# A two-layer hybrid decoder trunk on eight cores: attention summed in PSUM, the mixer's second half as one pipeline by tile, and the dense layer in two halves

## What is computed

```python
for layer in range(2):
    mod = silu(c) @ w_mod[layer] + b_mod[layer]          # 1024 x 6144, f32
    shift_m, scale_m, gate_m, shift_f, scale_f, gate_f = split(mod, 6)
    h = rms_norm(x, norm_mix) * (1 + scale_m) + shift_m
    q, k, v, rq, rk, rv, rg = split(h @ w_in[layer])     # 512 512 512 256 256 512 512
    # A: 8 heads of 64, three branches (window, dilation) = (128,1) (512,4) (2048,16)
    #    branch: p = exp(q k^T / 8 + bias); o = p v / sum(p); merged by softmax of log sum(p)
    # B: 4 heads, chunkwise retention in chunks of 128: inner + cross, state * decay + k^T v,
    #    GroupNorm per head, times silu(rg)
    x = x + gate_m * (concat(attn, ret) @ w_out[layer])
    h = rms_norm(x, norm_ffn) * (1 + scale_f) + shift_f
    f = swiglu(h, 1024 -> 2816 -> 1024)                  # layer 0, dense
        or top-2-of-8 experts swiglu(h, 1024 -> 3584 -> 1024)   # layer 1
    x = x + gate_f * f
```

## Time and profile before

| what | value |
|---|---|
| times of three executions | 4713.21, 4617.8, 4628.58 us |
| median | 4628.58 us |
| the profiled execution's own time | 4578.78 us |
| its span on the slowest core (core 0) | 4577.1 us |
| spans of the eight cores | 4534.5 to 4577.1 us |
| busy share of that span | PE 70%, DVE 37%, ACT 25%, POOL 17% |

### The profile page before, as it was taken

One profiled execution on the slowest core, in us unless ns is written; L12 is line 12 of the kernel. 1 busy time (PEld: TensorE's weight loads), 2 busy tenths in 40 slices (PEclk: granted clock), 3 DMA queues, 4 the chain that ended last, 5 costly groups with the idle time before them and its releaser, 6 DMA issues.

```text
span 4577.1 us, 59941 instructions; the slowest of 8 cores (4534.5 to 4577.1 us)
## 1 busy us (share of the span) xinstructions
PE 3189.4 (70%) x20346; PEld 1754.7 (38%) x20355; DVE 1694.2 (37%) x2545; ACT 1146.6 (25%) x2003; POOL 760.9 (17%) x668
## 2 busy tenths in 40 slices
PE   3677654556899966677455552669976788889876
PEld 1233343423343422333334222325543545455543
DVE  0488854333133335888544325112111212121211
ACT  2244432313110112444233032111111213021211
POOL 0100011120035460000111300201121111111120
PEclk9676666767899987766666775779998999999998
DMA  5311010013411122100110150897787969595966
GB/s 171 82 14 12 4 17 8 8 19 115 74 28 28 24 72 60 14 9 5 17 13 3 20 205 24 139 148 123 115 140 111 158 90 163 95 161 89 150 97 98
DMA packets 278861, 334.36 MB, mean 73 GB/s; under 512 B 67823, under 2 KB 205167, under 8 KB 278480
## 3 DMA queue, kind: packets, MB, share of 16 engines
q0 software_dynamic: 243696, 254.15, 37.7%
q1 hardware_dynamic: 34788, 75.30, 4.8%
HBM read 505.93 MB, written 36.96 MB: 119 GB/s over the span
## 4 chain that ended last, share of the span: by engine, by line
PE 51%; DVE 14%; DMA 13%; issue 9%; ACT 8%; POOL 3%; another core or an unknown queue 1%; DVEq 1%; ACTq 0%; POOLq 0%; SPq 0%; PEldq 0%
PE ps L1245 12%; PE ps L1273 10%; PE ps L931 7%; DMA s_w2s<-moe_w 4%; PE ps L450 3%; DMA s_ring<-moe_w 3%; POOL s_x L500 3%; PE ps L535 3%; PE ps L585 2%; DVE s_acc L707 2%; PE ps L680 2%; PE ps L657 2%; DVE s_hbf L477 1%; DVE s_acc L691 1%; ACT s_sa L1248 1%
## 5 line engine op out<-in xcount | busy, mean ns | idle before, releaser
L1245 PE MATMUL ps<-s_hgT,s_ring 128*128 128x0 bf16 (+1 forms) x5824 | 849.5, 307 | 228.4 <-DVE s_gT L1249 100.6
L1245 PEld LDWEIGHTS ps<-s_hgT,s_ring 128*128 128x128 bf16 x5824 | 552.9, 101 | 526.1 <-issue 293.2
L1249 DVE TENSOR_TENSOR s_gT<-ps,s_sa 128x384 bf16<-128x384 f32 (+1 forms) x364 | 233.0, 640 | 846.0 <-ACT s_sa L1248 798.9
L1273 PE MATMUL ps<-s_w2s,s_gT 128*128 128x512 bf16 x2072 | 460.0, 386 | 69.3 <-DMA s_w2s<-moe_w 68.9
L1248 ACT ACTIVATE s_sa<-ps 128x384 bf16<-128x384 f32 (+1 forms) x364 | 199.3, 556 | 527.0 <-PE ps L1245 484.2
L1273 PEld LDWEIGHTS ps<-s_w2s,s_gT 128*128 128x128 bf16 x2072 | 204.8, 99 | 321.9 <-issue 86.0
L931 PE MATMUL ps<-s_hT,s_w 128*128 128x512 bf16 x1408 | 307.0, 381 | 21.2 <-DMA s_w<-ffn_w 21.2
L450 PE MATMUL ps<-s_wm,s_cact_rep 128*128 128x512 f32 x384 | 191.7, 657 | 129.8 <-DMA s_wm<-w_mod 128.8
L1248 ACT ACT_TABLE_LOAD x56 | 71.8, 1283 | 755.5 <-PE ps L1245 746.0
L500 POOL TENSOR_TENSOR s_x<-s_x,s_tmpf 128x1024 f32<-128x1024 f32 x96 | 221.8, 2342 | 189.0 <-DVE s_tmpf L495 189.0
L594 DVE RECIPROCAL s_rsb<-s_rsb 128x512 f32<-128x512 f32 x64 | 214.5, 3351 | 91.8 <-ACT s_rsb L592 91.8
(11 more groups left out here) (219 smaller groups left out, 4354.8 us busy)
## 6 DMA issues: line engine op xcount, KB each, us to landing
s_ring<-moe_w POOLq DMA_DIRECT2D x112, 1024.0 KB, 18.5
s_w2s<-moe_w POOLq DMA_DIRECT2D x56, 1024.0 KB, 26.9
s_wm<-w_mod SPq DMA_DIRECT2D x24, 2048.0 KB, 9.4
s_w<-ffn_w POOLq DMA_DIRECT2D x10, 1024.0 KB, 10.8
s_x<-x SPq DMA_DIRECT2D x4, 2048.0 KB, 9.1
out<-s_x SPq DMA_DIRECT2D x4, 2048.0 KB, 7.9
s_wqkv<-w_in POOLq DMA_DIRECT2D x24, 256.0 KB, 4.4
s_w2s<-ffn_w POOLq DMA_DIRECT2D x5, 1024.0 KB, 8.5
```

The source lines that it names most:

```text
L1245: ins = e.matmul(o, lhsT=ring[s_][:, kc, j * 128:(j + 1) * 128], rhs=r, start=(kc == 0), stop=(kc == 7))
L1249: k.op("dve", lambda e: e.tensor_tensor(out=gT[:, fc, c0:c0 + width], in0=ps[:, bb, 0:width], in1=sa[z][:, 0:width], op=ALU.mult), reads=[ ...
L1273: ins = e.matmul(ps[:, b0 + hf, :], lhsT=gT[:, fc, b * 128:(b + 1) * 128], rhs=w2s[:, fc, hf * 512:(hf + 1) * 512], start=(fc == 0), stop= ...
```

## The change

The program is written anew from the setup to the router; the MoE's loop over expert tiles stays. Memory is no longer handed out by scopes with barriers: `place` puts each buffer at a fixed offset, and the helper makes it wait for whatever shared its bytes, so the barriers between stages are gone. x is not kept in SBUF. It is read and written by tile through DRAM (`load_x`, `residual`).

- **Setup.** Only the shift and scale of the first norm are computed ahead (8 loads of 1 MB, 32 f32 matmuls of 32 columns each, at four column places, L441). All 20 other blocks of w_mod are worked off on DVE inside layer 0's attention, eight [128x512] instructions a block (`mod_half`), and go through DRAM (`modscr`). The norm is one pipeline of square sum, apply, transpose.
- **Attention.** v is projected once for all heads in natural layout, laid beside a block of 64 ones per pair of heads, and the dilated copies are fetched through DRAM (`vscr`). Per head 19 batches of up to 512 columns: `scores`, exp, product in place, and `pv`, one matmul that yields 64 rows of p v and 64 rows of sums and accumulates all three branches in PSUM banks 0 to 3. `finish` forms the reciprocal as exp(-ln) on ACT, two instructions a bank, and one product on DVE. The projections of the next pair of heads are put between the batches, with the root as exp(-ln/2).
- **Mixer's second half.** One loop over tiles does project, rotate, transpose, state, inner, outer, GroupNorm, gate, transpose, output projection, residual, norm and transpose, each some iterations behind the one before. The mean of GroupNorm is taken out of the weights ahead (`wst`). For layer 1 the router's logits are in the same loop.
- **Dense layer.** Two halves of 1024 tokens: `up` for all 22 blocks, then `down` over all 22 accumulated in PSUM, followed by residual and norm. w1 and w3 are loaded twice, w2 once.
- **MoE.** The first tile always belongs to expert 0; its six ring buffers and seven down buffers are issued before the router's sorting.

```diff
@@ attention @@
-                            k.op("dve", lambda e: e.reciprocal(out=rsb[:, z, :], in_=rsb[:, z, :]), reads=[Brs[z]], writes=[Brs[z]])
+                k.op("act", lambda e: e.activation(out=rsb[:, y, :], in_=ps[:, 7, :], func=AF.Ln, bias=float(64 * EPS)), reads=[PB[7]], writes=[Brsb[y]])
+                k.op("act", lambda e: e.activation(out=rsb[:, y, :], in_=rsb[:, y, :], func=AF.Exp, scale=-0.5), reads=[Brsb[y]], writes=[Brsb[y]])
...
-                        k.op("dve", lambda e: e.tensor_tensor(out=dst, in0=dst, in1=pov, op=ALU.add), reads=[PB[ob], Bacc], writes=[Bacc])
+                for q, (lhs, bank, c0, d, n, o_) in enumerate(work):
+                    last = i == nb_ - 1 and all(w_[1] != bank for w_ in work[q + 1:])
+                    ins = e.matmul(ps[:, bank, c0:c0 + (n - 1) * d + 1:d], lhsT=lhs, rhs=pr[:, y, o_:o_ + n], start=False, stop=last)
...
+        def finish(c, hh):
+            num = slice(64 * hh, 64 * hh + 64)
+            den = slice(64 - 64 * hh, 128 - 64 * hh)
+            for bank in range(4):
+                y = bank % 2
+                k.op("act", lambda e: e.activation(out=rec[num, y, :], in_=ps[den, bank, :], func=AF.Ln), reads=[PB[bank]], writes=[Brec[y]])
+                k.op("act", lambda e: e.activation(out=rec[num, y, :], in_=rec[num, y, :], func=AF.Exp, scale=-1.0), reads=[Brec[y]], writes=[Brec[y]])
+                k.op("dve", lambda e: e.tensor_tensor(out=mixT[num, c, bank * 512:(bank + 1) * 512], in0=ps[num, bank, :], in1=rec[num, y, :], op=ALU.mult),
...
+            for hh in range(2):
+                pend = None
+                for i in range(nb_ + 2):
+                    if i < nb_:
+                        scores(c, hh, bts[i], i)
+                    if pend is not None:
+                        pend()
+                        pend = None
+                    elif fill and i % 5 == 1 and i < nb_:
+                        pend = proj(c + 1, *fill.pop(0))
...
+                    if i >= 2:
+                        pv(c, hh, bts[i - 2], i - 2)
@@ mixer, its one loop @@
+        for i in range(NT + 9):
+            at(i, 1, turn_qk)
+            at(i, 1, state)
+            at(i, 2, inner)
+            at(i, 4, gated)
+            at(i, 3, outer)
+            at(i, 5, turn_ret)
+            at(i, 6, outproj)
...
+            at(i, 7, norm_a)
+            at(i, 8, norm_b)
+            at(i, 0, project)
+            at(i, 0, evacuate)
@@ ffn @@
-            load13(0)
-            load2(0)
-            for gi in range(len(groups)):
+        load13(0)
+        load13(1)
+        for gi in range(n):
+            load2(gi)
+        n2 = None
+        for half in range(2):
+            for g in range(n):
+                gi = half * n + g
+                up(gi)
+                if gi + 2 < 2 * n:
+                    load13(gi + 2)
@@ moe @@
+        for g in range(3):
+            load13(0, g)
+        for g in range(FG):
+            load2(0, g)
...
-                load2(i, g)
+                if i > 0:
+                    load2(i, g)
...
-        set_expert(0)
         gather(0)
-        for g in range(3):
-            load13(0, g)
         set_shapes(0)
```

1715 lines of the change are left out of this document (898 added, 817 removed).

## The result

The kernel after took 4327.88 us in the median of 4 runs (4326.1 to 4433.98), the kernel before 4670.9 beside it on the same chip: a ratio of 0.936, with a 95% interval of 0.933 to 0.939. The direction was right. The size was not: 3700 us was forecast, and 4328 lies above the range, which ended at 3960.

A forecast was written before the change was run, and what follows sets the result against it. Only the dense layer and expert tiles were taken as PE-bound; DVE bounded attention, a chain of waiting stages the mixers' second halves. Eight stage terms summed to 3664 us, plus 1.1% for the median 3704, stated as 3700; range 3440 to 3960.

The forecast's parts named there:

- 52 us of waits. 466 + 52 + 16 = 535: Dense layer and second norm: PE's matmuls 466 us, waits for weights at the start 52, drained pipe ends 16.
- Tables switch: Rival in attention: Ln and Exp do not share a table, loads add 328 us, median 4035; chance 0.04.
- some 20 us by the rate of w_mod: Setup: the 24 bias table copies ahead of x's second half, 4.7 MB each way, adding 19 to reach 105 us.
- 38 a head for the 6.7 heads that carry blocks: Attention, layer 0: 38 us a head with w_mod blocks, 28 for the rest, 290 in a stage of 362.
- 5.5 us, so 44: Attention: the first pair's eight projections, serial through one bank, at 5.5 us each, 44 us together.
- 27 for six heads: Attention, layer 1: ACT's 23.3 us plus some 4 between heads, 20 for the last pair; 274 for the stage.
- 9600 columns of scores (4.2): Attention: PE's score matmuls of one head take 4.2 us, within 21 us of PE work at the full clock.
- 15 to 16 us: Mixer's second half, layer 0: time of one full loop iteration, against 11.5 with full overlap; stage 300 us with setup.
- walking the two queues: Mixer loop: following PE's and DVE's orders through one iteration, PE waiting about 2 us for `gated`, gives 15 to 16 us.
- The loops chain: Rival: mixer iterations take PE plus DVE, 22 us, and attention 40 us a head; median 3930; chance 0.18.
- 116 ahead of it: MoE: 105 us from mixer's end for loads ahead of the gathers, plus 11 for gathers and transposes, before the first tile.
- The lower clock: Rival: PE's work, about 2510 us at the full level, runs at 1.2 GHz, 5270 us with idle time; chance 0.02.

The follow-up runs named there:

- the last experiment: First two score batches of each head put ahead of the previous head's finish, against the combined kernel with the later modulation matmul: least run 3892.8 us, without it 3880 to 3891.

## Why the prediction was right or wrong, point by point

- **Dense layer: right in sum, in part by luck.** "52 us of waits. 466 + 52 + 16 = 535"; 538 was measured. PE's busy time came as priced, 473 for 466: here it has long, uninterrupted work, and prices of the earlier trace rows apply as they stand. The wait at the third group was 21.6 us and not 52; 18.5 before the first matmul and 21 of short waits, where 16 had been put, made up for it.
- **No table loads: right.** The rival "Tables switch" falls. Up to the router ScalarE loads a table twice in the setup (L428, L543), ahead of each mixer's Silu and once ahead of layer 1's attention; none lies between Ln and Exp, though they alternate throughout attention.

```profile
L927 ACT ACT_TABLE_LOAD x2 | 2.6, 1283 | 2.7 <-PE ps L907 2.7
...
L725 ACT ACT_TABLE_LOAD x1 | 1.3, 1283 | 0.6 <-PE ps L724 0.6
```

  The Trainium skill ("ScalarE: Activation LUTs", Table sets: the hidden batching unit) says that tables are loaded by set and that one set holds both exp and ln; the trace agrees with it. The last row is layer 1's only load for attention, 1.3 us for 32 projections and eight heads.
- **Setup: mis-sized.** "some 20 us by the rate of w_mod", bounded at 125 for the stage. The copies took 90 us: 24 at 3.8, 192 KB each. The term had a rate measured on 2 MB loads, and no account of the helper's rule, by which each copy waits for the one before. The run with the copies behind x let attention start 75 us earlier.
- **Attention of layer 0: a missing wait and a missing cost.** "38 a head for the 6.7 heads that carry blocks" counted VectorE and the bytes of w_mod. The changed kernel took 69 a head. The bias row's place behind 2 MB on SP's queue is some 105 us of it (by the run). The blocks' f32 matmuls were left out of PE's sum altogether: 80 records of about 1.05 us at the lower clock, 76 us of PE; taking them away gave 29 us on core 1, and moving the block's matmul two batches later 48 more. In both layers the first pair's serial projections took 57 us and not "5.5 us, so 44", at a granted clock of 0.70 in layer 1.
- **Attention of layer 1: ScalarE wasn't the bound.** "27 for six heads" by ScalarE's 23.3; measured 37.5, with PE busy 258 of 300 us and ScalarE 164. The term that failed is "9600 columns of scores (4.2)". At the full level a head has 8 batches of step 1 at about 0.34 us, seven of step 4 at 0.55 and four of step 16 at 1.08: 10.9 us, 6.7 more, or 54 us of the 98 that the layer's heads are longer: some 35 for the step and 18 because even a batch with step 1 takes 0.34 and not 0.22. Taking the step out of q gave 22.5 of them back. The 64 short value matmuls were taken at 4.9 us; sixteen in 0.55 make 2.2, but the step-4 values cost twice their price, which cancels. The other 44 us have no run of their own; the rows show a pause of 3.4 us at each head and the lower level for some 10 us behind it, and the last experiment moved neither.
- **Mixer loops: the overlap failed.** "15 to 16 us" and "20"; measured 20.5 and 26 to 27.5, with 38 to 39 in the iteration with the router's logits. The prices were right: with the order changed and nothing removed, the loops ran at 11.3 to 13.9 and 18.0 to 19.7, at or below my forecast. The step that failed is "walking the two queues". In layer 0 it had the right engines but gave PE a wait of "about 2 us"; the rows show 7.0, since VectorE begins its 11 us of residual, norm and rotation only behind PE's output projection, and PE needs the end of them; the lower clock came on top. In layer 1 the walk also missed a third and a fourth queue: ScalarE's copies, which free PE's banks, and POOL's subtraction stand behind work that waits for VectorE (105 us, or 95 when the subtraction was moved). Of the rivals, "The loops chain" named this mechanism and nearly its size (22 us).
- **The MoE: right on the core that was forecast.** The window ahead of the tile came as 106 us ("116 ahead of it"). The tile's 220 in place of "155" and 4 is core 1's, whose first tile has more work; its PE was busy 213.5 of 220 us at a clock of 1.00, so nearly nothing was waited for. On core 0, for which the forecast was made, the tile took 162 us and the other tiles 1457.8 ("1453"). That the loads delay the gather is shown: 24 us of this stage on core 1.
- **The lower clock** as a rival of its own was far off, with 0.81 over the core's span. It was present as an amplifier in every stage with pauses: 0.59 in layer 0's heads, 0.77 in the loop, and 0.89 in the same loop once PE hardly paused. The forecast had named "under 0.8 in the loops" as a sign of being wrong, and it came.

In sum, of 660 us too little some 75 are the copies, 180 the modulation blocks' waits and matmuls, over 50 in each layer the price of the score matmuls, 160 the order in the loops, 30 what stands ahead of the first head, and 16 the MoE's windows, where core 1's tiles stand against core 0's. The rest, some 80 to 90 us, is mostly attention's pauses at the lower clock, for which no run stands.

## What to carry to other kernels

A small load is late by everything that stands ahead of it on its queue, the waits of that queue included: when work is moved, write down per queue what stands in front of each instruction that somebody waits for, for all engines and not only the two busiest. Look too at which buffers a helper takes for one: a shared name turned 24 copies into a chain of 90 us. If an older tile's cheap copy frees a bank, it must not stand in line behind the youngest tile's chain; an order that puts "what others wait for" first was worth 200 us here without removing an instruction. Price a matmul from a row with its own type and its own access pattern, in the state of clock that its stage will have.

## What the runs showed of the hardware that was not expected

- A step in a matmul's moving operand costs time: four of 128 columns took 1.15 us with step 16 and 0.47 with step 1; two of 256 took 0.62 with step 4 and 0.41 without. Step 4 in the output costs as much: 0.61 against 0.40 us for four of 128. With step 16 sixteen matmuls of 32 columns took 0.63 us and 0.56 without.
- A single copy of 192 KB from DRAM to DRAM took 3.8 us, each begun after the one before had landed.
- An f32 matmul of 512 columns is two records, of 1.05 us each in layer 0's heads (granted clock 0.59) and of 0.59 in the median of 384 before (L450). A bf16 one took 0.47 at the lower level (1.9 us for four).
- Removing waits is repaid twice: in the mixer's loop of layer 0 PE's busy time for the same records fell from 220.6 us in 332 to 192.1 in 251, with the granted clock rising from 0.77 to 0.89.
